# Gate columns of a pooling mixer as seven block products per pair, trailing sums one column later

## The chip, the cores and the metric

The kernel runs on one core of a Trainium2 chip. The metric is device time in microseconds (us) of one execution; the time before is the median of three runs. TensorE (PE in the rows) multiplies, VectorE (DVE) and ScalarE (ACT) prepare its operands and take its results out of PSUM, SyncE (SP) issues the loads. Each of these engines works its own list of instructions in order and waits at semaphores for the others.

## The reference, cut to what matters

Two blocks of a network follow each other on 512 tokens with 1024 features. The change is in the first layer of the second block, the pooling mixer:

```
u = h @ w_in                       # 512 x 4096: 2048 values, 2048 gates
v, gate = split(u, 2)
for g, w in enumerate((2, 4, 8, 16)):          # four groups of 512 channels
    c = cumsum(v)[group g]; cnt = min(pos + 1, w)
    p[g] = (c - c shifted by w tokens) / cnt - v[group g]     # trailing mean minus token
m = p[g] @ w_grp[g] * scale
y = (m * silu(gate)) @ w_out
```

h is the RMS norm of the residual with a gain per feature.

## The kernel before, in words

**Three matmuls per product.** Every float32 operand is split into a high part, rounded to fp32r by ScalarE, and a low part, the rest, by a subtraction on VectorE. A product is high times high, high times low and low times high (`three`, L649 to L651). Activations lie in HH and HL with features on partitions, weights in WH and WL, four slots of 1024 columns each. A weight unit (128 x 1024, 512 KB) lands in one of five places of RAW, ScalarE copies it to WH (`hi_to`, L2375), VectorE subtracts (`lo_to`, L1371) and frees the place in RAW for the next load.

**The pooling mixer** works group after group, g from 0 to 3. Per group TensorE does four value columns ("pv", 128 output channels x 512 tokens over all 1024 features: 24 matmuls with 512 moving columns), four gate columns ("pg", the same shape) and the group product ("pm", 48 such matmuls). In group 0 the values are done in halves of 256 tokens while the second half of h is still being made. For each value column ScalarE copies the PSUM bank to VP (L2819), VectorE makes the trailing sum (`window`, g + 1 additions of a tile and its shifted self, L1898, each of which waits for the one before, then one scaled subtraction L1903 and two short instructions on the first 16 tokens), ScalarE rounds the result (L2809) and VectorE takes its low part (L1913). There is one VP and one result tile PP, so the four windows of a group take turns with ScalarE. A gate column goes through a sigmoid on ScalarE (L2827) and a multiplication on VectorE (L1923). The low part of a window and the multiplication of a gate are put off (`late`) and issued at the next `flush`.

**What sets the order.** Each engine has its own program that walks over the same columns; `column(evac)` issues the splits of the next units and then, at the eighth step, what evac does. A split of unit n + 2 stands in column n, ahead of that column's evacuation.

**The boundary behind fc2** (`boundary`) makes h for the mixer: TensorE transposes two token tiles at a time (L645); for the other two boundaries, out and pout, ScalarE writes the whole value to tile E (`whole`, L2483 or L2485), rounds it to HH (L2502), and VectorE subtracts (L1506). Behind fc2 both read PSUM directly, with the gain in the instruction (L2508, L1508), and E isn't written.

**Seven block products** are in use already in the fc1 stage. A pair of columns of 128 outputs over 1024 features and 512 tokens is taken as 2 x 2 blocks and done with seven products instead of eight (`half_product`, L990 to L992), each 12 matmuls with 256 moving columns. The sums of activation blocks are made once from E (`hidden_sums`, L1769 to L1775, four instructions of 1024 columns), rounded (`hidden_sum`, L2715) and given low parts in ER (`hidden_low`, L1784). Per pair four sums of weight blocks (`weight_sum`, 512 columns) and seven splits of 512 columns are made (L2735 on ScalarE, L1825 on VectorE). The products accumulate in PSUM: some are copied out by ScalarE (L2747, L2750), and VectorE adds three (L1838); a bank's next product waits until that is done. The hgrn value columns behind pout use such products too, with the same helpers; their weight splits are L2865 and L2010.

## Time and profile before

| | |
|---|---|
| median of 3 runs | 1404.72 us (1404.55 to 1405.58) |
| profiled execution | 1405.39 us, of which 1403.6 us from first to last instruction |
| TensorE busy | 1391.3 us (99%) |
| VectorE, ScalarE busy | 981.9 us (70%), 648.3 us (46%) |
| granted TensorE clock | 0.998 of full speed |
| pooling groups 1, 2, 3 begin at | 641.4, 696.1 and 750.8 us |

Matmuls overlap in the rows (one with 512 moving columns is shown with 0.39 us and the next begins well before it ends), so the pace of TensorE is read from start to start. The same holds for VectorE and ScalarE: an instruction that doesn't wait for its predecessor begins before that one's end.

### The profile page before, as it was taken

Reading aid. Unit: us, or ns where it says so; the run is one execution under the profiler, and the core shown is the slowest. Engines: PE = TensorE matmul, PEld = TensorE weight load, DVE = VectorE, ACT = ScalarE, POOL = GpSimd, SP = SyncE. Lnnn points to the kernel's source line nnn. Section 1 sums busy time; section 2 is a strip of 40 time slices with the busy share of each in tenths; the row PEclk is TensorE's granted clock in tenths of the full one; section 3 lists DMA queues with packets and bytes.
Section 4 is the critical chain, followed back from the end, with each engine's and each line's share of the span. In section 5 each row is a group of like instructions: output and inputs, shape, how many; then the busy total and the mean of one; then the engine's idle time right before and its main releaser. Section 6 shows DMA issues by size and latency. Waiting matters only on the chain.

```text
span 1403.6 us, 22088 instructions
## 1 busy us (share of the span) xinstructions
PE 1391.3 (99%) x8666; PEld 1191.6 (85%) x8666; DVE 981.9 (70%) x1922; ACT 648.3 (46%) x1268; POOL 0.2 (0%) x4
## 2 busy tenths in 40 slices
PE   8999999999999999999999999999999999999998
PEld 7888888999998888888888888988888888888886
DVE  7887776799953335655476535499788889888645
ACT  6423355567762324542342323575345555556441
POOL 0000000000000000000000000000000000000000
PEclk9999999999999999999999999999999999999999
DMA  9656441244333224032332234213322222221221
GB/s 359 220 177 250 152 157 70 95 163 154 111 115 99 97 94 161 32 105 91 93 117 75 91 107 148 76 43 112 117 91 76 76 76 78 74 76 61 76 75 60
DMA packets 43734, 158.00 MB, mean 113 GB/s; under 512 B 4848, under 2 KB 5232, under 8 KB 43632
## 3 DMA queue, kind: packets, MB, share of 16 engines
q1 hardware_dynamic: 43344, 156.39, 32.8%
q8 instruction: 69, 1.13, 0.3%
q14 instruction: 33, 0.27, 0.1%
q10 hardware_dynamic: 288, 0.21, 0.0%
HBM read 154.48 MB, written 2.10 MB: 112 GB/s over the span
## 4 chain that ended last, share of the span: by engine, by line
PE 97%; DVE 1%; issue 1%; DMA 0%; ACT 0%; SPq 0%; DVEq 0%; ACTq 0%
PE PS L649 26%; PE PS L651 26%; PE PS L650 26%; PE PS L990 2%; PE PS L992 2%; PE PS L991 2%; PE PS L1046 2%; PE PS L1048 2%; PE PS L1049 2%; PE PS L1147 1%; PE PS L1151 1%; PE PS L645 1%; PE PS L1139 1%; PE PS L1079 1%; PE PS L1160 0%
## 5 line engine op out<-in xcount | busy, mean ns | idle before, releaser
L649 PE MATMUL PS<-HH,WH 128*128 128x512 f32 (+1 forms) x880 | 337.3, 383 | 0.0
L651 PE MATMUL PS<-HH,WL 128*128 128x512 f32 (+1 forms) x880 | 332.8, 378 | 0.0
L650 PE MATMUL PS<-HL,WH 128*128 128x512 f32 (+1 forms) x880 | 332.5, 378 | 0.0
L2375 ACT ACTIVATE WH<-RAW 128x1024 fp32r<-128x1024 f32 x176 | 185.3, 1056 | 133.2 <-PE PS L651 87.0
L1371 DVE TENSOR_TENSOR WL<-RAW,WH 128x1024 fp32r<-128x1024 f32 x176 | 213.8, 1219 | 18.5 <-ACT WH L2375 18.1
L651 PEld LDWEIGHTS PS<-HH,WL 128*128 128x128 f32 x880 | 165.6, 188 | 31.4
L649 PEld LDWEIGHTS PS<-HH,WH 128*128 128x128 f32 x880 | 165.6, 188 | 30.7
L650 PEld LDWEIGHTS PS<-HL,WH 128*128 128x128 f32 x880 | 165.7, 188 | 29.3
L649 PE MATMUL PS<-WH,ZH 128*128 128x512 f32 x400 | 155.9, 390 | 0.0
L651 PE MATMUL PS<-WH,ZL 128*128 128x512 f32 x400 | 155.7, 389 | 0.0
L650 PE MATMUL PS<-WL,ZH 128*128 128x512 f32 x400 | 155.6, 389 | 0.0
L1422 DVE TENSOR_TENSOR ZL<-Z,ZH 128x512 fp32r<-128x512 f32 x52 | 35.6, 691 | 136.4 <-ACT ZH L2440 136.4
L2440 ACT ACTIVATE ZH<-Z 128x512 fp32r<-128x512 f32 x52 | 32.4, 632 | 149.2 <-PE PS L651 149.2
L651 PEld LDWEIGHTS PS<-WH,ZL 128*128 128x128 f32 x400 | 75.1, 188 | 15.7
L649 PEld LDWEIGHTS PS<-WH,ZH 128*128 128x128 f32 x400 | 75.1, 188 | 15.5 <-ACT Z L2750 0.2
L650 PEld LDWEIGHTS PS<-WL,ZH 128*128 128x128 f32 x400 | 75.1, 188 | 15.5
L990 PE MATMUL PS<-HH,WH 128*128 128x256 f32 x192 | 54.4, 283 | 0.3 <-DVE Z L1838 0.3
L992 PE MATMUL PS<-HH,WL 128*128 128x256 f32 x192 | 54.3, 283 | 0.0
L991 PE MATMUL PS<-ER,WH 128*128 128x256 f32 x192 | 54.3, 283 | 0.0
L2062 DVE RECIPROCAL DG<-W 128x96 f32<-128x96 f32 (+1 forms) x64 | 48.9, 815 | 0.0
L2467 ACT ACTIVATE TMP<-X 128x1024 f32<-128x1024 f32 x18 | 19.0, 1056 | 47.8 <-DVE X L1486 29.9
L649 PE MATMUL PS<-WH,HH 128*128 128x512 f32 x96 | 39.0, 407 | 2.0 <-DVE RAW L1331 2.0
(351 smaller groups left out, 2625.6 us busy)
## 6 DMA issues: line engine op xcount, KB each, us to landing
RAW<-in_w_fc SPq DMA_DIRECT2D x64, 512.0 KB, 3.5
RAW<-in_hgrn_in SPq DMA_DIRECT2D x56, 512.0 KB, 3.3
RAW<-in_pool_in SPq DMA_DIRECT2D x40, 512.0 KB, 3.3
RAW<-in_ada SPq DMA_DIRECT2D x36, 512.0 KB, 4.5
RAW<-in_w_in SPq DMA_DIRECT2D x26, 512.0 KB, 5.1
RAW<-in_pool_out SPq DMA_DIRECT2D x16, 512.0 KB, 3.3
RAW<-in_hgrn_out SPq DMA_DIRECT2D x16, 512.0 KB, 3.3
Z<-in_ada SPq DMA_DIRECT2D x12, 512.0 KB, 4.4
```

The costliest lines, as they stand in the source:

```text
L649: e.matmul(out, wh, xh, start=first, stop=False)
L650: e.matmul(out, wh, xl, start=False, stop=False)
L651: return e.matmul(out, wl, xh, start=False, stop=last)
L990: e.matmul(out, wh[:, k, :], xh[k], start=fresh and k == 0, stop=False, skip_group_check=True)
L991: e.matmul(out, wh[:, k, :], xl[k], start=False, stop=False, skip_group_check=True)
L992: mm = e.matmul(out, wl[:, k, :], xh[k], start=False, stop=k == 3, skip_group_check=True)
L1046: e.matmul(out, xh[k][:, cols], wh, start=k == 0 and p in (1, 2, 7), stop=False, skip_group_check=True)
L1371: e.tensor_tensor(lo, raw(i), hi.bitcast(F32), ALU.subtract).then_inc(taken.sem, taken(i))
L1422: e.tensor_tensor(lo, Z[:, k, :], hi.bitcast(F32), ALU.subtract).then_inc(zlo.sem, zlo(z))
L2062: e.reciprocal(i8[:, n, l], w8[:, n, l]).then_inc(own.sem, own("iw", h, i))
L2375: e.activation(place(s)[0], raw(i), ACT.Copy).then_inc(whi.sem, whi(s))
L2440: e.activation(z_place(z)[0], Z[:, k, :], ACT.Copy).then_inc(zhi.sem, zhi(z))
```

## The change

The fc2 boundary now goes through E as the other two do, and `hidden_sums`, `hidden_sum` and `hidden_low` are called for it in group 0. In groups 1 to 3 the four gate columns become two pairs with seven products each, 14 per group (list `POOLED`; the second number of a pair is the pair of columns). Windows 0, 1 and 2 of these groups stand in the evacuation of the following value column, window 3 behind the second product. The additions of a window are as before.

```diff
+POOLED = [(p, 2 * g + n) for g in range(3) for p, n in
+          ((1, 0), (7, 0), (6, 0), (2, 0), (4, 0), (5, 0), (1, 1), (7, 1), (3, 0), (6, 1), (2, 1), (5, 1), (4, 1), (3, 1))]
...
+        def pooled_bank(p, q):
+            return gate_bank(1, {7: 2, 4: 2, 2: 3}.get(p, q % 2))
...
+            def pooled_product(m):
+                i, q = POOLED[m]
+                b = pooled_bank(i, q)
+                claim(b)
+                if i in (3, 5, 6, 7) and q == 0:
+                    e.wait_ge(hidden_high.sem, hidden_high.of("fc2", i))
+                e.wait_ge(taken.sem, taken.of("pooled", m))
...
+                for k in range(4):
+                    e.matmul(out, wh[:, k, :], xh[k], start=fresh and k == 0, stop=False, skip_group_check=True)
+                    e.matmul(out, wh[:, k, :], xl[k], start=False, stop=False, skip_group_check=True)
+                    mm = e.matmul(out, wl[:, k, :], xh[k], start=False, stop=k == 3, skip_group_check=True)
...
-                for j in range(4):
+                for j in range(0 if g else 4):
                     run(column(("pg", g, j), gate_bank(g, j)))
+                if g:
+                    for m in range(14 * g - 14, 14 * g):
+                        pooled_product(m)
+                    p.unit += 4
...
-            boundary("fc2", VEC[:, V_NG0:V_NG0 + 8])
+            boundary("fc2", None)
...
+            def pooled_low(m):
+                i, q = POOLED[m]
+                if i == 5 and q % 2 == 0:
+                    pooled_sum(3, q + 1)
+                if i == 1 and q % 2:
+                    pooled_sum(2, q)
+                if i == 7 and q % 2:
+                    pooled_sum(4, q)
+                if i == 3 and q % 2 == 0:
+                    pooled_sum(1, q + 1)
+                e.wait_ge(copied.sem, copied.of("pooled", m))
+                hi, lo = pooled_place(m)
+                e.tensor_tensor(lo, pooled_source(m), hi.bitcast(F32), ALU.subtract).then_inc(
+                    taken.sem, taken("pooled", m))
...
+            def first_pooled(g, j):
+                q = 2 * g - 2
+                if j == 0:
+                    pooled_sum(3, q)
+                    pooled_sum(2, q)
+                if j == 1:
+                    window(g, 0)
+                    pooled_sum(4, q)
+                    pooled_low(7 * q)
+                    pooled_low(7 * q + 1)
+                if j == 2:
+                    window(g, 1)
+                    pooled_sum(1, q)
+                    pooled_low(7 * q + 2)
+                    pooled_low(7 * q + 3)
+                if j == 3:
+                    window(g, 2)
+                    pooled_low(7 * q + 4)
...
-                    run(halved([[], [lambda j=j: window(0, j) for j in range(4)]]))
+                    run(halved([[], [lambda j=j: window(0, j) for j in range(4)]], lambda: hidden_sums("fc2")))
+                    for j in range(4):
+                        run(column(lambda: pool_gate(0, j)))
+                        hidden_low("fc2", (7, 6, 5, 3)[j])
                 else:
                     for j in range(4):
-                        run(column(lambda: window(g, j)))
-                for j in range(4):
-                    run(column(lambda: pool_gate(g, j)))
+                        run(column(lambda: first_pooled(g, j)))
+                    for m in range(14 * g - 14, 14 * g):
+                        n = m % 14
+                        if n + 5 < 14:
+                            pooled_low(m + 5)
+                        if n:
+                            pooled_taken(*POOLED[m - 1])
+                        if n == 1:
+                            window(g, 3)
+                        if n == 6:
+                            flush()
+                        if n in (7, 11):
+                            pooled_silu(g, (7, 11).index(n))
+                        if n == 10:
+                            p.unit += 4
+                            lo_to(p.unit + 1)
...
+            def pooled_copied(i, q):
+                b = pooled_bank(i, q)
+                if i in (1, 7, 6):
+                    e.wait_ge(*banks.made(("pooled", i, q)))
+                    if q:
+                        e.wait_ge(*banks.taken(("pooled", {1: 2, 7: 5, 6: 4}[i], q - 1)))
+                    e.activation({1: C1, 7: C7, 6: C2}[i], PS[b][:, 0:256], ACT.Copy).then_inc(banks.free[b], 1)
...
+                    for m in range(14 * g - 14, 14 * g + 1):
+                        n = m - 14 * g + 14
+                        if n:
+                            pooled_copied(*POOLED[m - 1])
+                        if n == 4:
+                            pool_high(g, 3)
+                        if n + 6 < 14:
+                            pooled_high(m + 6)
+                        if n in (6, 10, 14):
+                            pooled_sigmoid(g, (6, 10, 14).index(n))
+                        if n == 9:
+                            p.unit += 4
+                            hi_to(p.unit + 2)
```

`pooled_sum` is `weight_sum` for the gate units (3, 2 and 4 write to TMP, 1 to RAW), `pooled_high` is ScalarE's rounding of half a unit, and `pooled_taken` adds a copied product to the bank of products 2, 4 and 5.

On VectorE in group 0, behind the last window (L1898 and L1962 are its addition, L1913 and L1977 its low part), before:

```order
L1898 TENSOR_TENSOR Z<-Z 128x512
L1903 SCALAR_TENSOR_TENSOR Z<-Z 128x496
L1905 TENSOR_TENSOR Z<-Z,CST 128x16
L1908 TENSOR_TENSOR Z<-Z 128x16
L1913 TENSOR_TENSOR ZR<-Z,PSP 128x512
L1371 TENSOR_TENSOR WL<-RAW,WH 128x1024
L1923 TENSOR_TENSOR Z<-Z,PS 128x512
L1371 TENSOR_TENSOR WL<-RAW,WH 128x1024
```

and in the same place after the change (L1433 is the split of a whole unit, L1848 is `hidden_low`, L1987 the gate's multiplication):

```order
L1962 TENSOR_TENSOR Z<-Z 128x512
L1967 SCALAR_TENSOR_TENSOR Z<-Z 128x496
L1969 TENSOR_TENSOR Z<-Z,CST 128x16
L1972 TENSOR_TENSOR Z<-Z 128x16
L1977 TENSOR_TENSOR ZR<-Z,PSP 128x512
L1848 TENSOR_TENSOR ER<-E,ZH 128x256 x2
L1848 TENSOR_TENSOR ER<-E,ZL 128x256 x2
L1433 TENSOR_TENSOR WL<-RAW,WH 128x1024
L1987 TENSOR_TENSOR Z<-Z,PS 128x512
```

Four short subtractions stand ahead of the split that the fourth gate column of group 0 needs.

On VectorE in group 3, from window 3 on, before (window, then splits of whole units and gates in turn):

```order
L1898 TENSOR_TENSOR Z<-Z 128x512 x4
L1903 SCALAR_TENSOR_TENSOR Z<-Z 128x496
L1905 TENSOR_TENSOR Z<-Z,CST 128x16
L1908 TENSOR_TENSOR Z<-Z 128x16
L1371 TENSOR_TENSOR WL<-RAW,WH 128x1024
L1913 TENSOR_TENSOR ZR<-Z,PSP 128x512
L1371 TENSOR_TENSOR WL<-RAW,WH 128x1024
L1923 TENSOR_TENSOR Z<-Z,PS 128x512
L1371 TENSOR_TENSOR WL<-RAW,WH 128x1024
```

and after the change (L1999, L2003, L2006 and L2009 are the weight sums 3, 2, 4 and 1, L2023 the split of half a unit, L2037 is `pooled_taken`):

```order
L1962 TENSOR_TENSOR Z<-Z 128x512 x4
L1967 SCALAR_TENSOR_TENSOR Z<-Z 128x496
L1969 TENSOR_TENSOR Z<-Z,CST 128x16
L1972 TENSOR_TENSOR Z<-Z 128x16
L2006 TENSOR_TENSOR TMP<-RAW,TMP 128x512
L2023 TENSOR_TENSOR WL<-TMP,WH 128x512
L2009 TENSOR_TENSOR RAW<-RAW 128x512
L2023 TENSOR_TENSOR WL<-RAW,WH 128x512
L2023 TENSOR_TENSOR WL<-TMP,WH 128x512
L2037 TENSOR_TENSOR Z<-PS,TMP 128x256
L2023 TENSOR_TENSOR WL<-RAW,WH 128x512
L2037 TENSOR_TENSOR Z<-PS,TMP 128x256
```

The second addition L2037 is that of product (4, 0); it frees the PSUM bank that product (7, 1), the eighth of the group, claims. Two sums and four splits stand between window 3 and it.

## Rows read from the trace of the kernel before

**Rows 1.** The page: TensorE's busy time, and the chain that ended last.
```profile
PE 1391.3 (99%) x8666; PEld 1191.6 (85%) x8666; DVE 981.9 (70%) x1922; ACT 648.3 (46%) x1268; POOL 0.2 (0%) x4
PE 97%; DVE 1%; issue 1%; DMA 0%; ACT 0%; SPq 0%; DVEq 0%; ACTq 0%
```

**Rows 2.** Timeline of TensorE: start us, us, engine, line, operation, out<-in, shape, count.
```profile
641.40 0.39 PE L649 MATMUL PS<-HH,WH 128*128 128x512 f32 x1
684.95 0.40 PE L649 MATMUL PS<-PSP,WH 128*128 128x512 f32 x1
```

**Rows 3.** Timeline of TensorE in the fc1 products.
```profile
339.93 0.28 PE L990 MATMUL PS<-HH,WH 128*128 128x256 f32 x1
342.81 0.28 PE L990 MATMUL PS<-HH,WH 128*128 128x256 f32 x1
```

**Rows 4.** Timeline of VectorE, pooling group 3, first window.
```profile
757.15 2.87 DVE L1898 TENSOR_TENSOR Z<-Z 128x512 f32<-128x512 f32 x4 [3.07 <-ACT Z L2819]
760.94 1.22 DVE L1371 TENSOR_TENSOR WL<-RAW,WH 128x1024 fp32r<-128x1024 f32 x1
```

**Rows 5.** Timeline of VectorE in the fc1 products.
```profile
293.28 0.69 DVE L1825 TENSOR_TENSOR WL<-TMP,WH 128x512 fp32r<-128x512 f32 x1
293.88 0.42 DVE L1838 TENSOR_TENSOR Z<-PS,TMP 128x256 f32<-128x256 f32 x1
294.21 0.68 DVE L1825 TENSOR_TENSOR WL<-RAW,WH 128x512 fp32r<-128x512 f32 x1
```

**Rows 6.** Timeline of ScalarE, pooling group 3.
```profile
761.96 0.60 ACT L2819 ACTIVATE Z<-PS 128x512 f32<-128x512 f32 x1 [3.90 <-PE PS L651]
762.45 0.62 ACT L2809 ACTIVATE PSP<-Z 128x512 fp32r<-128x512 f32 x1
```

**Rows 7.** Busy us and instructions per engine, two stretches.
```profile
core 0: us, PE busy (x) PEld busy (x) DVE busy (x) ACT busy (x) POOL busy (x), PEclk, DMA share, GB/s
320.00:360.00 40.00, 40.00 (x336) 40.00 (x335) 36.19 (x61) 29.03 (x60) 0.00 (x0) 1.00 0.43 145
700.00:760.00 60.00, 60.00 (x265) 49.45 (x264) 35.79 (x58) 19.51 (x25) 0.00 (x0) 1.00 0.32 103
```

**Rows 8.** Timeline of TensorE, a wait in the fc1 products.
```profile
297.76 0.39 PE L990 MATMUL PS<-ZH,WH 128*128 128x256 f32 x1 [0.77 <-ACT TMP L2747]
297.98 0.28 PE L991 MATMUL PS<-ER,WH 128*128 128x256 f32 x1
```

**Rows 9.** Timeline of TensorE, group 0: first matmul of its fourth gate column.
```profile
624.82 0.39 PE L649 MATMUL PS<-HH,WH 128*128 128x512 f32 x1
```

**Rows 10.** Timeline of VectorE, group 0.
```profile
608.28 0.70 DVE L1898 TENSOR_TENSOR Z<-Z 128x512 f32<-128x512 f32 x1
621.13 0.69 DVE L1913 TENSOR_TENSOR ZR<-Z,PSP 128x512 fp32r<-128x512 f32 x1 [0.70 <-ACT PSP L2809]
622.08 1.23 DVE L1371 TENSOR_TENSOR WL<-RAW,WH 128x1024 fp32r<-128x1024 f32 x1 [0.26 <-ACT WH L2375]
```

**Rows 11.** Timeline of ScalarE, group 0.
```profile
621.00 1.04 ACT L2375 ACTIVATE WH<-RAW 128x1024 fp32r<-128x1024 f32 x1
621.95 0.58 ACT L2827 ACTIVATE Z<-PS 128x512 f32<-128x512 f32 x1
```

**Rows 12.** Timeline of TensorE, second transposes behind fc2 and behind pout.
```profile
593.35 0.33 PE L645 MATMUL PS<-CST,Z 128*128 128x128 f32 x1
904.03 0.38 PE L645 MATMUL PS<-CST,Z 128*128 128x128 f32 x2
```

**Rows 13.** Timeline of VectorE behind pout.
```profile
910.73 1.23 DVE L1769 TENSOR_TENSOR E<-E 128x1024 f32<-128x1024 f32 x1
915.64 1.22 DVE L2010 TENSOR_TENSOR WL<-RAW,WH 128x1024 fp32r<-128x1024 f32 x1
916.78 1.43 DVE L1784 TENSOR_TENSOR ER<-E,ZR 128x256 fp32r<-128x256 f32 x4
```

**Rows 14.** Timeline of ScalarE behind pout.
```profile
914.50 1.34 ACT L2715 ACTIVATE ZR<-E 128x256 fp32r<-128x256 f32 x4 [3.35 <-DVE E L1773]
```

More of the change, by code:

```diff
@@ L80, in slot_list @@
 def slot_list():
-    slots, before, last, ring, first, vfirst = [], [], {}, 0, None, None
+    slots, before, last, ring, first, vfirst, pooled = [], [], {}, 0, None, None, []
     for s, i in enumerate(GEMM):
@@ L96, in slot_list @@
                 ring = (first[0] + len(PRODUCTS)) // 2
+            continue
+        if name == "pool_in" and n >= 10 and 4 <= n % 10 < 8:
+            if n % 10 == 4:
+                pooled.append((2 * ring, dict(last)))
+            slots.append(None)
+            before.append(None)
+            if n % 10 == 7:
+                for m in range(14):
+                    last[(pooled[-1][0] + m) % (2 * NS) // 2] = "pooled", 14 * (len(pooled) - 1) + m
+                ring += 7
             continue
@@ L120, in slot_list @@
         last[slot] = s
-    return slots, before, first, vfirst
-SLOT, BEFORE, PFIRST, VFIRST = slot_list()
+    return slots, before, first, vfirst, pooled
+SLOT, BEFORE, PFIRST, VFIRST, GFIRST = slot_list()
 def product_half(m):
@@ L397, in operand @@
                     return h, [l[:, i, :] for i in range(4)]
+                if p == 3 and stage == "fc2":
+                    h = [ZR[:, 30 + i // 2, 256 * (i % 2):256 * (i % 2) + 256] for i in range(4)]
+                    return h, [l[:, i, :] for i in range(4)]
                 if p != 3:
@@ L546, in ready @@
         def ready(stage, p, k):
-            if stage == "fc2" and k >= 4:
-                return banks.taken((stage, "t", p, k - 4))
             return hlo.sem, hlo.of(stage, p, k)
@@ L1001, in tensor_program @@
             rows("fc2", 32)
+            def pooled_product(m):
[5 more added lines that the diff above has]
+                e.wait_ge(taken.sem, taken.of("pooled", m))
+                wh, wl = (x.rearrange("p (k c) -> p k c", k=4) for x in pooled_place(m))
+                xh, xl = operand(i, "fc2")
+                out, fresh = PS[b][:, 0:256], i in (1, 2, 7)
+                for k in range(4):
+                    e.matmul(out, wh[:, k, :], xh[k], start=fresh and k == 0, stop=False, skip_group_check=True)
+                    e.matmul(out, wh[:, k, :], xl[k], start=False, stop=False, skip_group_check=True)
+                    mm = e.matmul(out, wl[:, k, :], xh[k], start=False, stop=k == 3, skip_group_check=True)
+                mm.then_inc(banks.full[b], banks.fill(("pooled", i, q), b))
+                wfree["pooled", m] = banks.made(("pooled", i, q))
             for g in range(4):
@@ L1421, in z_low @@
                     e.wait_ge(*banks.made(("product", 7 - (z - 8), FG - 1)))
+                if ZSTAGE[z] == 2 and z - 40 < NZ:
+                    e.wait_ge(*banks.made(("pooled", {2: 7, 0: 6, 1: 5}[ZSLOT[z]], 5)))
                 e.tensor_tensor(lo, Z[:, k, :], hi.bitcast(F32), ALU.subtract).then_inc(zlo.sem, zlo(z))
@@ L1924, in pool_gate, with pooled_sum @@
                 late.append(last)
+            def pooled_sum(i, q):
+                a, b = pooled_units(q)
+                b11, b21, b12, b22 = (raw(n)[:, c:c + 512] for n in (a, b) for c in (0, 512))
+                if i != 1 and q:
+                    e.wait_ge(taken.sem, taken.of("pooled", POOLED.index(({3: 7, 2: 6, 4: 4}[i], q - 1))))
+                if i == 3:
+                    e.wait_ge(*landed(b))
+                    e.tensor_tensor(PT[3], b22, b12, ALU.subtract).then_inc(own.sem, own("pooled", 7, q))
+                elif i == 2:
+                    e.wait_ge(*landed(a))
+                    e.wait_ge(own.sem, own.of("pooled", 7, q))
+                    e.tensor_tensor(PT[2], PT[3], b11, ALU.add).then_inc(own.sem, own("pooled", 6, q))
+                elif i == 4:
+                    e.wait_ge(own.sem, own.of("pooled", 6, q))
+                    e.tensor_tensor(PT[4], b21, PT[2], ALU.subtract).then_inc(own.sem, own("pooled", 4, q))
+                else:
+                    e.wait_ge(own.sem, own.of("pooled", 7, q))
+                    e.tensor_tensor(b12, b12, b11, ALU.subtract).then_inc(own.sem, own("pooled", 5, q))
@@ new lines, in pooled_silu @@
+            def pooled_silu(g, j):
+                e.wait_ge(gate.sem, gate.of("pg", g, j))
+                e.tensor_tensor(Z[:, 16 + j, :], Z[:, 16 + j, :], pooled_gate(j), ALU.mult).then_inc(
+                    own.sem, own("pg", g, j))
+            def first_pooled(g, j):
[16 more added lines that the diff above has]
+                    pooled_low(7 * q + 4)
@@ L2435, in z_high @@
                     e.wait_ge(*banks.made(("product", 7 - (z - 8), FG - 1)))
+                if ZSTAGE[z] == 2 and z - 40 < NZ:
+                    e.wait_ge(*banks.made(("pooled", {2: 7, 0: 6, 1: 5}[ZSLOT[z]], 5)))
                 if ZSLOT[z] == NZ:
@@ L2710, in hidden_sum @@
                 x, h = quarter(E, k, t), operand(i, stage)[0]
-                if stage == "out" and i == 3:
-                    e.wait_ge(*banks.made(("fc1", FS - 1)))
+                if i == 3 and stage != "pout":
+                    e.wait_ge(*banks.made(("fc1", FS - 1) if stage == "out" else ("pv", 0, 3)))
                 e.wait_ge(own.sem, own.of("sum", stage, i))
@@ L2834, in scalar_program @@
                     run(halved([[], [lambda j=j: pool_values(0, j) for j in range(4)]]))
+                    pool_high(0, 3)
+                    for j in range(4):
+                        run(column(lambda: pool_gate(0, j)))
+                        hidden_sum("fc2", (7, 6, 5, 3)[j])
                 else:
```

91 lines of the change are left out of this document (70 added, 21 removed).

## The prediction, made before the changed kernel ran

> **What bounds the kernel now.** I read the page first: TensorE is busy 1391.3 of 1403.6 us, and the chain that ended last is TensorE for 97% [rows 1]. So the time is the number of matmuls times their pace, and a change pays only by what it takes off TensorE and by waits that it doesn't bring there. Then the timeline of TensorE, start to start. Between 641.40 and 684.95 lie the eight columns of group 1, 192 matmuls with 512 moving columns: 43.55 / 192 = 0.2268 us each [rows 2]. In the fc1 products 24 matmuls with 256 columns take 342.81 - 339.93 = 2.88 us, 0.120 each, 1.44 per product [rows 3]. Last, the timelines of VectorE and ScalarE, which must feed the new products. VectorE has room in the mean (35.79 of 60 us busy in group 2 and the start of group 3 [rows 7]), but a product wait is decided by its place in an in-order list, so I count the list.
>
> **What TensorE saves.** Four gate columns are 96 matmuls x 0.2268 = 21.78 us; 14 products are 168 x 0.120 = 20.16 us. 1.62 us less per group, **4.9 us** in three groups. The number of instructions grows by 216; group 0, the values and the group product stay.
>
> **A rule that speaks against it.** The rows give a short matmul 0.53 of a long one. The Trainium skill, "TensorE: Matmul & The Clock Gate", section "Back-to-back issue gap", gives a stream of weight loads and matmuls about 131 ns at 512 columns and about 81 at 128. By these, as an estimate, 168 matmuls at 81 or more (13.6 us) replace 96 at 131 (12.6), and the change loses at least 1 us per group before any wait. The trace has neither level; I go by the rows.
>
> **Durations of the helpers, start to start.** VectorE: a split or sum of 512 columns 293.88 - 293.28 = 0.60 (0.605 in longer runs), an addition out of PSUM with 256 columns 0.33, 0.42 until it is finished [rows 5]. The four additions of a window take 2.87 to the end of the last, (2.87 - 0.69) / 3 = 0.725 each since each waits for the one before; the whole window of group 3 is 760.94 - 757.15 = 3.79, so w = 0.89 + 0.725 (g + 1): 2.34, 3.07 and 3.79 us in groups 1, 2, 3 [rows 4]. ScalarE: a bank of 512 columns 0.49, the rounding behind it 0.62 until it is finished [rows 6]. A stopped TensorE restarts with one matmul of 0.22 in place of 0.12 [rows 8]: 0.1 us more per wait.
>
> **Groups 1 to 3: the wait of the eighth product.** Time from the group's start. The products begin at 21.78, the eighth, (7, 1), is due at 21.78 + 7 x 1.44 = 31.86. Its PSUM bank is that of (4, 0), freed by a VectorE addition. What stands ahead of that on VectorE: column 1 of the values ends at 10.89, ScalarE starts on it 0.29 later and has rounded window 0 by 11.18 + 0.49 + 0.62 = 12.29. From 12.32 on VectorE has no pause: low part of window 0, window 1, a sum and two splits, low part, window 2, then split, sum, split, sum, split, low part, window 3, sum, split, sum, split, split, the addition of (2, 0), a split, the addition of (4, 0). That is 17 instructions x 0.605 = 10.28, three windows, and 0.33 + 0.42 + 0.03: together 12.32 + 11.06 + 3w = 23.4 + 3w.
> - Group 3: 34.8, 2.9 late. With the restart 3.05. (The third product waits 0.3 for the copy of the first, which ScalarE reaches late; that lies inside the 2.9.)
> - Group 2: 32.6, 0.73 late, with the restart 0.85.
> - Group 1: 30.4, but the split ahead of window 3 waits for its rounding, which ScalarE does behind column 3 (21.78 + 0.29 + 0.49 + 0.52 + 0.62 = 23.7). From there 8 x 0.605 + 2.34 + 0.78 = 7.96, so 31.7: 0.16 early, no wait.
>
> Bounds for this term: nothing if the list is as little late as in the fc1 products, where the longest wait shown is 0.77 [rows 8]; and one more 0.085 per instruction if VectorE needs the full 0.69 shown instead of 0.605, as below. I take the ledger, since its durations come from the same instructions.
>
> **The twelfth product.** (5, 1) claims the bank that ScalarE copies for (6, 1). That copy stands behind the rounding of the second pm unit, whose place in WH is free only when (6, 1) itself is done. So: end + 0.2, 0.95 [rows 11] for the rounding, 0.4 for the copy, 0.06 = 1.6 against the 1.44 of (2, 1) in between: 0.15 plus restart, **0.25 per group**, between nothing and 0.5. Later products, the two sigmoids at the end and the split of the second pm unit fit: about 3.6 us after the last product (5.2 in group 2, where eight short instructions on the next layer's bounds stand ahead) against the 5.57 until it is needed.
>
> **Group 0: the split behind `hidden_low`.** The fourth gate column starts at 624.82 [rows 9]; its weight split starts at 622.08 [rows 10], done 1.5 us before. After the change three things push it.
> - The boundary through E and the four sums. Behind pout the sums start 910.73 - 904.03 = 6.70 after the second transposes and take 915.64 - 910.73 = 4.91 [rows 12, 13]. Behind fc2 that makes 593.35 + 6.70 = 600.05, about 0.45 more for the ScalarE rounding (1.04 [rows 11]) that the split ahead of the sums waits for, that split 1.15, sums 4.91, two splits 2.29: the first window starts at 608.85, not at 608.28 [rows 10], 0.57 late. The four windows alternate with ScalarE, so this stays.
> - ScalarE then does rounding, sigmoid and, new, four copies of a hidden sum: 621.95 + 0.57 + 0.48 = 623.0, and 1.34 for four [rows 11, 14], 624.35.
> - VectorE waits for these and subtracts, four in 1.34 (one alone 0.42, 1.43 to the end of the fourth [rows 13]), to 625.7; only then the split, 1.22 [rows 13], 626.95.
>
> TensorE wants it at 624.82: **2.15 us late**, 2.25 with the restart. Bounds: 1.0 if the ScalarE copies overlap, 3.0 if the boundary is as slow as the one with a shift. The next splits are in time. The boundary itself costs TensorE nothing: it waits for the token norms, as before.
>
> **Sum.** Waits 2.25 + 0.25 + (0.85 + 0.25) + (3.05 + 0.25) = 6.9, saving 4.9: **2.0 us more**. Against the profiled execution (1403.6 span, 1405.39 with what lies around it) that is 1407.4; against the median 1404.72 it is **1406.7**.
>
> **Rivals.**
> - *VectorE keeps pace.* For it: in the fc1 products TensorE is busy 40.00 of 40 us with VectorE at 36.19 [rows 7], and the pooling groups load VectorE less in the mean. Against: no window of 3.8 us stands in that list. Then only the twelfth products wait, 0.75 in all, and the time is 1404.7 - 4.9 + 0.75 = 1400.6.
> - *Slower: VectorE pays full durations.* Place: the same lists. If a sum or split here needs its shown 0.69 [rows 5] because each waits for another engine's semaphore, 17 x 0.085 = 1.4 us come on top in groups 3 and 2, 0.7 in group 1, 0.2 in group 0: 1404.7 + 2.0 + 3.7 = 1410.4. It decides from a spacing of about 0.64, which gives 1408.3. For it: the window additions do pay (0.725). Against: the splits in [rows 5] wait for ScalarE too and are 0.60 apart.
> - *The short matmul costs its shown share.* If the pace went as the durations, 0.28 to 0.39 [rows 2, 3], 168 x 0.72 x 0.2268 = 27.4 per group in place of 21.8, 17 us in all, 1429 with the waits. The page named above leans that way, the trace doesn't.
> - *Only part is done.* The order shows 216 more matmuls and none of the gate columns left in groups 1 to 3, so I give it nothing.
>
> **How the numbers follow.** Forecast 0.6, VectorE keeps pace 0.14, full durations 0.25, shown share 0.01. A measurement of this kernel tells about 0.2% (2.8 us) from no change, so faster is under 1401.9 and slower over 1407.5. The forecast's own range is 1404.8 to 1408.6 (group 0 between 1.0 and 3.0, group 3 between 2.2 and 4): of its 0.6, 0.43 lie within the bound, 0.16 above, 0.01 below. Of 0.14, 0.11 is faster and 0.03 the same; of 0.25, 0.20 is slower and 0.05 the same. Faster 0.12, same 0.51, slower 0.37. The range, with about one in ten left out on each side, is 1402.5 to 1409.8.
>
> **What would show it.** The changed profile should have TensorE idle before a 512-column matmul near 625 us, released by VectorE's whole-unit split, about 2 us; idle before a product with 256 columns some 32 us after the start of groups 2 and 3, released by VectorE's addition from PSUM, near 0.8 and 2.9 us, and none or almost none in group 1; a short one about four products later, released by ScalarE's copy to TMP. Products at 1.44 us each between. I am wrong if these waits are missing (then the first rival), if VectorE's splits stand 0.69 apart (the second), or if TensorE waits elsewhere, at the fc2 transposes above all.

## The result

| | before | after |
|---|---|---|
| median | 1404.72 us | 1408.67 us (11 executions, 1407.87 to 1409.56) |
| profiled execution | 1405.39 us, span 1403.6 | 1409.56 us, span 1407.8 |
| ratio to before | | 1.0027, interval 1.0019 to 1.0035 |

The change costs 3.95 us by these medians, and 3.8 by the ratio. The forecast was 1406.7, which is 2.0 us more than before. The result lies in the range of 1402.5 to 1409.8, and beyond the 0.2% within which I had put my largest chance. The direction and the places were right. The size was not: nearly half of the loss is something that the sum had no term for.

The page of the changed kernel, the rows that answer to [rows 1]:

```profile
PE 1389.9 (99%) x8882; PEld 1199.9 (85%) x8882; DVE 1023.4 (73%) x2014; ACT 676.5 (48%) x1354; POOL 0.2 (0%) x4
PE 91%; DVE 6%; ACT 1%; issue 1%; DMA 0%; SPq 0%; ACTq 0%; DVEq 0%
```

TensorE is busy 1.4 us less and the span is 4.2 us longer, so it now stands still for some microseconds. In the chain VectorE went from 1% to 6%. Where it is shows in busy time by stretch, about group 0 and then groups 1, 2 and 3 (columns as in [rows 7]). First the kernel before, where all four stretches look alike:

```profile
596.00:640.00 44.00, 44.00 (x244) 38.37 (x243) 24.30 (x43) 16.79 (x25) 0.00 (x0) 1.00 0.27 90
...
750.00:810.00 60.00, 60.00 (x265) 49.40 (x264) 39.16 (x56) 19.19 (x26) 0.00 (x0) 1.00 0.29 92
```

and the changed one:

```profile
596.00:640.00 44.00, 41.90 (x224) 36.03 (x223) 32.53 (x63) 22.69 (x46) 0.00 (x0) 0.96 0.25 84
640.00:700.00 60.00, 59.95 (x342) 52.62 (x341) 43.37 (x71) 25.94 (x45) 0.00 (x0) 1.00 0.30 97
700.00:750.00 50.00, 49.43 (x295) 43.91 (x295) 41.46 (x77) 23.08 (x40) 0.00 (x0) 1.00 0.30 97
750.00:810.00 60.00, 57.51 (x323) 50.55 (x323) 46.63 (x77) 24.37 (x43) 0.00 (x0) 0.97 0.29 96
```

Two things are to be seen. TensorE stands still for 2.1, 0.05, 0.57 and 2.49 us. And the granted clock, the third number from the end, was 1.00 in all four stretches before and is 0.96 and 0.97 in the two stretches with the long waits. The chip took the clock down there.

The first of them, in TensorE's timeline (the wait in brackets, then the durations), which answers to [rows 9]:

```profile
626.25 0.50 PE L690 MATMUL PS<-HH,WH 128*128 128x512 f32 x1 [2.10 <-DVE WL L1433]
626.59 0.39 PE L691 MATMUL PS<-HL,WH 128*128 128x512 f32 x1
626.82 0.46 PE L692 MATMUL PS<-HH,WL 128*128 128x512 f32 x1
627.07 0.63 PE L690 MATMUL PS<-HH,WH 128*128 128x512 f32 x1
...
630.06 0.57 PE L691 MATMUL PS<-HL,WH 128*128 128x512 f32 x1
630.46 0.39 PE L692 MATMUL PS<-HH,WL 128*128 128x512 f32 x1
```

From start to start the wait costs 2.26 us over the usual pace and the restart 0.11. From 627.07 to 630.46 eight matmuls take 3.39 us where eight at 0.227 take 1.82: 1.57 us more. In windows of one microsecond the granted clock reads so:

```profile
625.00:626.00 1.00, 0.00 (x0) 0.00 (x0) 1.00 (x2) 1.00 (x4) 0.00 (x0) 1.00 0.00 0
627.00:628.00 1.00, 1.00 (x4) 0.74 (x4) 1.00 (x4) 1.00 (x4) 0.00 (x0) 0.50 0.53 168
...
631.00:632.00 1.00, 1.00 (x6) 0.83 (x5) 1.00 (x2) 0.00 (x0) 0.00 (x0) 1.00 0.87 352
```

TensorE stood still at the upper level (2.4 GHz), took up work again, fell to the lower one (1.2 GHz) 0.8 us after the restart and came back while it was busy. The eighth product of group 3 shows the same with 256 columns, where the spacing grows from 0.12 to 0.21 us half a microsecond after the restart:

```profile
786.86 0.38 PE L1056 MATMUL PS<-ZH,WH 128*128 128x256 f32 x1 [2.27 <-DVE Z L2037]
787.09 0.28 PE L1057 MATMUL PS<-ER,WH 128*128 128x256 f32 x1
...
787.32 0.31 PE L1056 MATMUL PS<-ZH,WH 128*128 128x256 f32 x1
787.44 0.41 PE L1057 MATMUL PS<-ER,WH 128*128 128x256 f32 x1
```

Time over the usual pace, in us, added up over all matmuls of a stretch:

| | forecast | waits and restarts | behind a fallen clock |
|---|---|---|---|
| group 0, fourth gate column | 2.25 | 2.37 | 1.57 |
| group 1, twelfth product | 0.25 | 0.31 | |
| group 2, eighth and twelfth | 0.85 + 0.25 | 0.79 + 0.30 | |
| group 3, third | in the next | 0.43 | |
| group 3, eighth and twelfth | 3.05 + 0.25 | 2.53 + 0.31 | 1.48 |
| sum | 6.9 | 7.04 | 3.05 |

Less 4.9 saved, the waits alone make 2.2 us, and with both falls 5.2 us. The measured median is between, 3.95. The span of this one execution is only 4.2 us longer because all before fc2's second transposes took 0.83 us less: they start at 592.52, not at 593.35 as in [rows 12]. Nearly all of that is a fall of the clock near the start of the kernel, far from the change. The trace of the kernel before has it:

```profile
17.85 0.47 PE L649 MATMUL PS<-WH,HH 128*128 128x512 f32 x1 [2.04 <-DVE RAW L1331]
...
19.43 0.63 PE L649 MATMUL PS<-WH,HH 128*128 128x512 f32 x1
...
20.00:21.00 1.00, 1.00 (x4) 0.81 (x3) 1.00 (x2) 0.97 (x3) 0.00 (x0) 0.50 1.03 410
```

TensorE waits 2.04 us there, and 1.2 us after the restart the clock is at its lower level. The changed kernel has the same wait of 2.04 us, and in this profile no fall behind it. From the restart (17.85 before, 17.75 after) to the first product with ZR (25.84 and 24.98) the fall costs 0.76 us, less than its slow matmuls, because the changed kernel's profile has a wait of 0.64 us behind them (until 21.82) and the other has none there.

### The profile page after: what moved, and what is told of

Its sections match the earlier page's. It is cut to its first block, busy times and chain, and to the rows that moved or that the text cites. A ratio compares the mean times of both kernels' runs of the same rounds, so it can differ in the third digit from the quotient of the medians.

```text
span 1407.8 us, 22809 instructions
## 1 busy us (share of the span) xinstructions
PE 1389.9 (99%) x8882; PEld 1199.9 (85%) x8882; DVE 1023.4 (73%) x2014; ACT 676.5 (48%) x1354; POOL 0.2 (0%) x4
## 4 chain that ended last, share of the span: by engine, by line
PE 91%; DVE 6%; ACT 1%; issue 1%; DMA 0%; SPq 0%; ACTq 0%; DVEq 0%
PE PS L690 23%; PE PS L692 23%; PE PS L691 23%; PE PS L1031 2%; PE PS L1033 2%; PE PS L1032 2%; PE PS L1108 2%; PE PS L1111 2%; PE PS L1110 2%; DVE Z L1962 1%; PE PS L1056 1%; PE PS L1209 1%; PE PS L1057 1%; PE PS L1058 1%; PE PS L1213 1%
## 5 line engine op out<-in xcount | busy, mean ns | idle before, releaser
L690 PE MATMUL PS<-HH,WH 128*128 128x512 f32 (+1 forms) x784 | 301.0, 384 | 2.1 <-DVE WL L1433 2.1
L692 PE MATMUL PS<-HH,WL 128*128 128x512 f32 (+1 forms) x784 | 296.2, 378 | 0.0
L691 PE MATMUL PS<-HL,WH 128*128 128x512 f32 (+1 forms) x784 | 296.0, 378 | 0.0
L2534 ACT ACTIVATE WH<-RAW 128x1024 fp32r<-128x1024 f32 x164 | 172.5, 1057 | 123.9 <-PE PS L692 77.1
L1433 DVE TENSOR_TENSOR WL<-RAW,WH 128x1024 fp32r<-128x1024 f32 x164 | 199.1, 1219 | 17.1 <-ACT WH L2534 16.7
L690 PEld LDWEIGHTS PS<-HH,WH 128*128 128x128 f32 x784 | 147.9, 189 | 29.6 <-DVE WL L1433 2.5
L692 PEld LDWEIGHTS PS<-HH,WL 128*128 128x128 f32 x784 | 148.0, 189 | 27.8
L691 PEld LDWEIGHTS PS<-HL,WH 128*128 128x128 f32 x784 | 148.2, 189 | 25.6
```

The source lines that it names most:

```text
L690: e.matmul(out, wh, xh, start=first, stop=False)
L691: e.matmul(out, wh, xl, start=False, stop=False)
L692: return e.matmul(out, wl, xh, start=False, stop=last)
L1433: e.tensor_tensor(lo, raw(i), hi.bitcast(F32), ALU.subtract).then_inc(taken.sem, taken(i))
L2534: e.activation(place(s)[0], raw(i), ACT.Copy).then_inc(whi.sem, whi(s))
```

## The experiments

All ratios are to the kernel before, timed in turn on the same chip. Its median was 1405.38 us beside the first four experiments, 1405.11 beside the waits put in by hand and the first repeat of the changed kernel, and 1405.48 beside the rest.

**One part of group 0 undone.** The blocks of `hidden_low` one column later:

```diff
                     for j in range(4):
                         run(column(lambda: pool_gate(0, j)))
-                        hidden_low("fc2", (7, 6, 5, 3)[j])
+                        if j:
+                            hidden_low("fc2", (7, 6, 5)[j - 1])
+                    hidden_low("fc2", 3)
```

> The changed kernel, with each block of hidden_low in group 0 issued one column later on VectorE, so that the weight split of the fourth gate column stands ahead of the first block. In the trace of the changed kernel TensorE waits 2.26 us there, restarts with 0.11 more, and the eight matmuls after it start 0.2 us further apart than usual (1.57 us together) while the granted clock is at its lower level. Theory A (the place in VectorE's list makes the wait, and the clock falls because of the wait): wait, restart and slow matmuls all go, 3.9 us less, 1404.7 us. Theory B (the wait goes, but the clock falls near 628 us anyway): 2.4 us less, 1406.3. Theory C (VectorE simply has too much to do there, the wait moves to a later column): within 1 us of the changed kernel, 1408.

Measured: 1405.73 us, ratio 1.0002 (0.9993 to 1.0011), so 3.5 us less than the changed kernel's 1.0027. VectorE in this kernel:

```profile
622.09 1.23 DVE L1433 TENSOR_TENSOR WL<-RAW,WH 128x1024 fp32r<-128x1024 f32 x1 [0.26 <-ACT WH L2536]
623.24 0.68 DVE L1987 TENSOR_TENSOR Z<-Z,PS 128x512 f32<-128x512 f32 x1
623.87 0.76 DVE L1848 TENSOR_TENSOR ER<-E,ZH 128x256 fp32r<-128x256 f32 x2
```

The split stands right behind the low part of the window again, as in [rows 10], and no wait is left in group 0. In the changed kernel it stood behind the four subtractions, and began 4.07 us behind that low part (L1977) and not 0.95, so 3.12 us later:

```profile
620.90 0.69 DVE L1977 TENSOR_TENSOR ZR<-Z,PSP 128x512 fp32r<-128x512 f32 x1 [0.70 <-ACT PSP L2962]
623.62 0.76 DVE L1848 TENSOR_TENSOR ER<-E,ZH 128x256 fp32r<-128x256 f32 x2 [2.03 <-ACT ZL L2868]
624.30 0.75 DVE L1848 TENSOR_TENSOR ER<-E,ZL 128x256 fp32r<-128x256 f32 x2
624.97 1.22 DVE L1433 TENSOR_TENSOR WL<-RAW,WH 128x1024 fp32r<-128x1024 f32 x1
```

VectorE idles 2.03 us for ScalarE's copies while a split that it could do waits in line. Theory C falls: nothing moved to a later column. Theory A and theory B differ only in the clock behind 628 us, which is up in this profile. Something else is to be seen: group 3 still has its wait of 2.44 us over the pace, in the profile with the clock up.

```profile
783.07 0.39 PE L1056 MATMUL PS<-ZH,WH 128*128 128x256 f32 x1 [2.28 <-DVE Z L2037]
...
783.53 0.29 PE L1056 MATMUL PS<-ZH,WH 128*128 128x256 f32 x1
```

The eleven executions lie in two clusters, five from 1403.96 to 1404.92 and six from 1405.73 to 1406.39; the profiled one belongs to the lower. So the same wait may have a fall behind it in one execution and none in the next. That is not shown: no execution of the upper cluster was profiled, and the fall near 20 us, which the profiled one doesn't have either, is a second thing that can differ (worth 0.8 us, where the clusters lie some 1.8 apart).

**Window 3 later.** Behind the addition of (4, 0) and (5, 0) instead of ahead of them:

```diff
-                        if n == 1:
-                            window(g, 3)
-                        if n == 6:
-                            flush()
+                        if n in (1, 13):
+                            flush()
+                        if n == 6:
+                            window(g, 3)
...
-                        if n == 4:
+                        if n == 11:
                             pool_high(g, 3)
```

> The changed kernel, with window 3 of groups 1 to 3 moved on VectorE from behind the second product's split to behind the addition of product (5, 0), its rounding on ScalarE behind the copy of the tenth product, and its low part behind the thirteenth step. Theory A (list place): the waits of the eighth product, 0.69 + 0.1 in group 2 and 2.43 + 0.1 in group 3, go, and with the latter about 1.5 us of slow matmuls behind it; the twelfth product's waits and the 0.33 at the third stay. 4.8 us less than the changed kernel, 1403.9. Theory B (slow matmuls are not due to the wait): 3.3 less, 1405.4. Theory C (VectorE has too much to do in group 3, its window of 3.8 us only shifts the wait to products 12 to 14 or to the group product): less than 1.5 us gained, 1407.2 or more.

Measured: 1404.2 us, ratio 0.9994 (0.9985 to 1.0002), 4.6 us less than the changed kernel. VectorE in group 3:

```profile
781.32 0.41 DVE L2037 TENSOR_TENSOR Z<-PS,TMP 128x256 f32<-128x256 f32 x1
781.65 0.67 DVE L2023 TENSOR_TENSOR WL<-RAW,WH 128x512 fp32r<-128x512 f32 x1
782.25 0.41 DVE L2037 TENSOR_TENSOR Z<-PS,TMP 128x256 f32<-128x256 f32 x1
782.59 2.85 DVE L1962 TENSOR_TENSOR Z<-Z 128x512 f32<-128x512 f32 x4
```

The waits of the eighth product are gone in both groups, and none came in their place: what is left in groups 2 and 3 is 0.31, 0.43 and 0.30 us. So the wait comes not from the amount of VectorE's work but from the place of 3.8 us of it. Group 0 keeps its 2.27 us wait, this time with a granted clock of 1.00 behind it in the profile. The time alone can't tell theory A from theory B (4.6 us less, where they say 4.8 and 3.3, and the two ratios leave 1.6 us either way); the trace shows that wait and slow matmuls are both gone.

**Both, and the rounding of the second pm unit behind the copy of (6, 1).**

```diff
                             p.unit += 4
-                            hi_to(p.unit + 2)
+                            hi_to(p.unit + 1)
+                        if n == 10:
+                            hi_to(p.unit + 2)
```

> Both of these moves, and ScalarE's rounding of the second unit of the group product behind the copy of the tenth product instead of ahead of it, so that the twelfth product's bank is free in time (three waits of 0.2 + 0.1). Theory A: 3.9 + 4.8 + 0.9 less than the changed kernel, 1399.1; with what stays (0.4 at the third product of group 3) it would be the 4.9 us saved on TensorE less 0.5, near 1400. Theory C: the waits come back elsewhere, 1404 or more.

Measured: 1400.75 us (five executions within 1399.96 and 1401.03), ratio 0.9969 (0.9956 to 0.9981). One wait is left in the four groups:

```profile
772.64 0.39 PE L1056 MATMUL PS<-ZH,WH 128*128 128x256 f32 x1 [0.17 <-ACT TMP L3003]
```

The twelfth products wait no more. The 4.9 us saved less 0.43 make 4.5; the ratio gives 4.4. The 3.9, 4.8 and 0.9 that I had added up to 1399.1 held both falls in full, which the median of the changed kernel doesn't.

**Work for TensorE in its waits.**

```diff
+            def fill(b, n):
+                claim(b)
+                for _ in range(n):
+                    e.matmul(PS[b][:, 0:256], HH[:, 0, 0:128], HH[:, 0, 0:256], start=True, stop=True,
+                             skip_group_check=True)
...
                 for j in range(0 if g else 4):
+                    if j == 3:
+                        fill(gate_bank(0, 3), 17)
                     run(column(("pg", g, j), gate_bank(g, j)))
...
                     for m in range(14 * g - 14, 14 * g):
+                        if m == 35:
+                            fill(pool_bank(3, 0), 19)
                         pooled_product(m)
```

> The changed kernel with work for TensorE in its two long waits: 17 matmuls of 256 columns into a PSUM bank that nobody reads, ahead of the fourth gate column of group 0 (2.0 of 2.26 us), and 19 ahead of the eighth product of group 3 (2.3 of 2.43 us). The lists of the other engines are unchanged, so the columns behind start when they did. Theory A (the clock falls because TensorE stands still): the granted clock stays at its upper level behind both places, 1.6 + 1.5 = 3.1 us less, 1405.6. Theory B (the clock falls for another reason, or from TensorE's load): no change, 1408.7, and the same eight slow matmuls.

Measured: 1406.88 us, ratio 1.0013 (1.0004 to 1.0022). The lists of the other engines are the same, the column and the product start as long after their predecessors as they did (to 0.03 us in group 0), and yet the time is 2.0 us less than the changed kernel's. Nine of eleven executions lie between 1406.56 and 1407.76; two took 3581 and 6526 us, for which I have no cause. TensorE in group 0:

```profile
624.06 0.39 PE L692 MATMUL PS<-HH,WL 128*128 128x512 f32 x1
624.29 2.19 PE L1048 MATMUL PS<-HH 128*128 128x256 f32 x17
626.57 0.50 PE L690 MATMUL PS<-HH,WH 128*128 128x512 f32 x1
626.90 0.39 PE L691 MATMUL PS<-HL,WH 128*128 128x512 f32 x1
```

With useless matmuls in the waits the clock stayed up behind both places. For group 0 one profile says little, since three of four profiles of the changed kernel have no fall there either; for group 3 all four have it. All nine usual executions lie below the fastest one of the changed kernel (1407.76 and 1407.87). So the fall in group 3 needs TensorE to stand still, and the falls are worth about 2.0 us in the changed kernel's median (the two ratios' intervals leave 0.3 to 3.7), not the 3.1 of its first profile.

**A wait put into the kernel before.** Ahead of the split of the fourth gate column of group 0, n subtractions into a tile that nobody reads (the expectations call them additions), with n = 4, 5 and 10; with 4:

```diff
                     e.wait_ge(whi.sem, whi.of(s))
+                    if UNITS[i][0] == "pool_in" and UNITS[i][1] == 7:
+                        for _ in range(4):
+                            e.tensor_tensor(S2[:, 16:PADW], raw(i)[:, 0:512], hi.bitcast(F32)[:, 0:512],
+                                            ALU.subtract).then_inc(own.sem, own())
+                            e.wait_ge(own.sem, own.n)
```

> The kernel before the change, with one wait put into it by hand: ahead of the weight split of the fourth gate column in group 0 VectorE does four additions on an unused tile (128x512, each waits for the one before, 0.725 us apart as in a window). The split was done 1.5 us before it was needed, so TensorE should stand still for 4 x 0.725 - 1.47 = 1.4 us, plus 0.1 of restart. If the wait costs only itself: 1.5 us more than before. If the granted clock falls behind a wait of this length: about 1.5 us on top in the executions in which it falls. The waits of 0.69 us in the changed kernel's traces show no fall, so I expect few falls or none: 1.5 us more, the executions within 1 us of each other.

> The same with five additions: TensorE should stand still for 5 x 0.725 - 1.47 = 2.15 us, as it does in group 0 of the changed kernel. In five profiles of kernels with waits of this size (two places each) the clock fell behind some and not behind others. If the fall comes with the wait, with a chance: 2.3 us more than before in one part of the executions and 3.9 in the other, in two clusters. If the clock has nothing to do with the wait: 2.3 us in all.

> The same with ten additions: a wait of 10 x 0.725 - 1.47 = 5.8 us. If the fall depends on how long TensorE stands still, the clock now falls in every execution, and all lie in one cluster: 5.9 us for wait and restart and 1.6 or more for slow matmuls, 7.5 to 8.5 us more than before. If it is independent of the wait's length, as with five additions: two clusters.

| n | wait in the profile | restart and slow matmuls | median | over before | executions |
|---|---|---|---|---|---|
| 4 | 1.45 us | 0.11 | 1406.65 | 1.54 (1.0010) | 1405.88 to 1406.95 |
| 5 | 2.18 us | 0.11 | 1407.69 | 2.58 (1.0018) | 1406.66 to 1408.63 |
| 10 | 5.81 us | 2.5 | 1413.9 | 8.8 (1.0064) | 1413.83 to 1414.22 |

With 1.45 us the wait costs itself, 1.56. With 5.81 us the clock is down before TensorE starts again:

```profile
629.00:630.00 1.00, 0.00 (x0) 0.00 (x0) 0.97 (x2) 0.00 (x0) 0.00 (x0) 0.64 0.00 0
630.00:631.00 1.00, 0.10 (x1) 0.10 (x1) 1.00 (x2) 0.00 (x0) 0.00 (x0) 0.50 0.00 0
635.00:636.00 1.00, 1.00 (x4) 0.81 (x3) 0.00 (x0) 0.00 (x0) 0.00 (x0) 0.50 0.98 229
636.00:637.00 1.00, 1.00 (x5) 0.79 (x5) 0.00 (x0) 0.00 (x0) 0.00 (x0) 0.94 0.90 348
```

and the five executions agree to 0.4 us, as the first theory had it. Their 8.8 us are somewhat above its 7.5 to 8.5. With 2.18 us no clear pair of clusters came out, only a spread of 2.0 us with a median 0.3 over the 2.28 that the profile without a fall shows.

**Further profiles of the same two kernels.**

> The changed kernel again, for a second profile and eleven more executions. Its waits must be the same to 0.05 us, since the lists are. If the slow matmuls come by chance of the execution, this profile may show them behind the wait of group 0, behind the eighth product of group 3, behind both or neither, and the time is 2.2 us over before plus 1.5 for each. If they belong to the kernel, they are in the same two places again.

> The changed kernel, one more profile: the waits of 2.26 and 2.44 us must be there again. Whether the matmuls behind them are slow was so once in group 0 and twice in group 3, of two profiles each; if chance of the execution decides, this differs from one profile to the next while the waits stay.

> As the one before: the same waits, and behind each the clock fallen or not.

> The kernel before with the wait of 2.18 us put in by hand, one more profile. In the first the clock stayed up. Its eleven executions reach from 1406.66 to 1408.63 us, 2 us, so some must have had the fall; this one shows it or not.

Measured: 1408.86 us (eight executions, ratio 1.0027, 1.0017 to 1.0037) for the first, and single executions of 1408.98, 1408.75 and 1407.51. In the changed kernel each wait came out the same to 0.02 us in all four profiles. TensorE's restart in group 0 in the third of them:

```profile
627.22 0.50 PE L690 MATMUL PS<-HH,WH 128*128 128x512 f32 x1 [2.10 <-DVE WL L1433]
...
628.02 0.40 PE L690 MATMUL PS<-HH,WH 128*128 128x512 f32 x1
```

Counted over all profiles with a wait of 2.2 to 2.5 us: in group 0 the clock fell behind one of seven (one of four in the changed kernel, none in window 3 later and in the two with five additions). It fell where the wait ended at 626.25, and not in the six where it ended between 627.0 and 627.5. In group 3 it fell in all four of the changed kernel, where the wait ends between 786.1 and 786.9, and not in the one where it ends at 783.1. So the length of the wait alone does not decide; the moment at which it comes may have a part. The profiles differ in one thing more: the one with the fall in group 0 has no fall near 20 us, and the six without have it. It is also why its wait ends almost 1 us earlier than in the repeats. Of the 14 profiles of all kernels, 11 have the fall near 20 us, and 3 of these 11 have it already at 14 to 15 us, behind a wait of only 0.9 us in a stretch where TensorE does small matmuls.

**The copy of the first product ahead of the rounding.** On ScalarE, behind all of the moves above:

```diff
+                        if n == 1:
+                            pooled_high(m + 5)
-                        if n + 6 < 14:
+                        if n and n + 6 < 14:
                             pooled_high(m + 6)
```

> The kernel with both moves and the later rounding of the second unit of the group product, and on ScalarE the copy of a group's first product ahead of the rounding of the seventh half instead of behind it. The last wait that its predecessor shows is the third product of group 3, 0.33 + 0.10 us. If that copy's place makes it, it goes: 0.4 us less than the predecessor's 0.9969 of before, about 1400.4 against a before of 1405.1, that is all of the 4.9 us that TensorE saves. If the rounding put off by 0.4 us is late for VectorE, a wait of a few tenths appears at products 7 to 9 instead.

Measured: 1400.35 us, ratio 0.9963 (0.995 to 0.9977). Group 3 and its values in this kernel:

```profile
750.00:810.00 60.00, 60.00 (x345) 52.89 (x344) 49.40 (x80) 26.08 (x45) 0.00 (x0) 1.00 0.34 106
```

The 0.4 us against the kernel before it is less than the two ratios can tell apart; that the wait of the third product is gone, the trace shows. TensorE stands still nowhere in the four groups, at the upper clock throughout, with VectorE at 49.40 of 60 us: more in the same time than in the changed kernel. This version beats both, by 5.1 and by about 9 us.

## Why the prediction came out as it did

**The saving was right.** From 666.38 to 686.84 group 1 does its 14 products, 20.46 us with a wait of 0.31 in them, so 20.15 against 20.16. The last kernel, which has no waits, is 0.37% under before: 5.1 us where the sum says 4.9. The pace behind it, as in [rows 2, 3]:

```profile
666.38 0.28 PE L1056 MATMUL PS<-HH,WH 128*128 128x256 f32 x1
666.50 0.28 PE L1057 MATMUL PS<-HL,WH 128*128 128x256 f32 x1
...
686.84 0.39 PE L690 MATMUL PS<-PSP,WH 128*128 128x512 f32 x1
```

The rival with the short matmul at its shown share is out with that. By the estimate from the figures of the Trainium skill, "TensorE: Matmul & The Clock Gate", section "Back-to-back issue gap", the change would have lost at least 1 us per group before any wait; the trace doesn't agree, with 0.120 and 0.227 us a matmul.

**The ledger of VectorE was right.** In group 3 it said that (4, 0) is added at 34.8 us from the start of the group. The products of that group begin at 773.93, which puts its start at 752.14, and the addition (the second L2037, 0.42 long) ends at 786.81, so 34.7. VectorE's rows there, which answer to [rows 4, 5], with window 3 ahead of the sums and splits:

```profile
778.67 2.86 DVE L1962 TENSOR_TENSOR Z<-Z 128x512 f32<-128x512 f32 x4
...
782.45 0.69 DVE L2006 TENSOR_TENSOR TMP<-RAW,TMP 128x512 f32<-128x512 f32 x1
...
786.39 0.42 DVE L2037 TENSOR_TENSOR Z<-PS,TMP 128x256 f32<-128x256 f32 x1
```

Group 2 came out at 32.5 for 32.6 (730.07 + 0.41 from 697.99), and in group 1 there is no wait, as said. Sums and splits stand 0.60 apart and not 0.69, so the rival of full durations did not happen, though its 1410.4 is a little nearer to the measured time (1.7 us off) than my forecast (2.0). A time that fits doesn't show a cause: the trace shows none of its spacing.

**Group 0 was right but for a tenth.** Its split was forecast for 625.7 in the time of the kernel before; it starts at 624.97 in an execution whose second transposes come 0.83 earlier than in [rows 12] (592.52), so at 625.8. The wait is 2.26 for 2.15. The boundary behind fc2 cost TensorE nothing, as said: its 16 second transposes take 1.73 us before (from 593.35) and 1.72 after (from 592.52), with no wait around them.

**The twelfth product was right** (0.31 for 0.25 each). ScalarE in group 1, where rows of the same two kinds as in [rows 6, 11] follow each other:

```profile
681.04 1.07 ACT L2534 ACTIVATE WH<-RAW 128x1024 fp32r<-128x1024 f32 x1 [0.17 <-PE PS L1058]
682.01 0.36 ACT L3001 ACTIVATE TMP<-PS 128x256 f32<-128x256 f32 x1
```

The rounding of the pm unit (L2534) waits for TensorE's tenth product, and the copy (L3001) stands behind it. That copy frees the bank for the twelfth product, which starts at 682.42. That wait and that of the third product of group 3 end when the experiments move what stands ahead of ScalarE's copy.

**The rival in which VectorE keeps pace** named about the time that the kernel has once places in VectorE's and ScalarE's lists are changed: 1400.6, against 1400.75 and 1400.35. That is in part luck, since its 0.75 for the twelfth products is not in those two. Against it I had put the window of 3.8 us in the list, and moving just that window took the waits of the eighth products away.

**The step that failed is the sum.** It read "Waits 2.25 + 0.25 + (0.85 + 0.25) + (3.05 + 0.25) = 6.9", and charged each wait with its length and 0.1 for one slow matmul. That was read off a wait of 0.77 us [rows 8], and I took over the small price without bounding the large one. The rows that I quoted don't show what follows a wait of 2 us, but the trace of the kernel before did: its wait of 2.04 us at 17.85 has the clock at 0.50 behind it, so the term could have been asked for. The missing term is the granted clock: 1.57 us in group 0 when it falls, 1.48 in group 3. As an estimate from the four profiles of the changed kernel, a fall in one of four and in four of four makes 0.25 x 1.57 + 1.48 = 1.9 us, and 2.2 + 1.9 = 4.1 where 3.95 was measured. The filled waits, without a fall in the profile, gave 1.8 us over before where the sum of waits gives 2.2.

**Profile by profile the terms add up.** From the span of the kernel before, 1403.6 with the fall near 20 us, I take the 4.9 saved, and 0.8 more where that fall is missing, and add the waits, restarts and slow matmuls that the trace shows in the four groups:

| profile | fall near 20 us | waits and restarts | behind falls | worked out | span |
|---|---|---|---|---|---|
| changed kernel, first | no | 7.0 | 3.05 | 1408.0 | 1407.8 |
| changed kernel, three repeats | yes | 7.1 | 1.5 | 1407.3 | 1407.1, 1407.2, 1407.0 |
| `hidden_low` later | no | 4.7 | 0 | 1402.6 | 1402.6 |
| window 3 later | yes | 3.7 | 0 | 1402.4 | 1402.4 |
| both and the rounding | yes | 0.4 | 0 | 1399.1 | 1399.0 |
| waits filled | no | 7.1 | 0 | 1405.0 | 1405.1 |
| copy of the first product ahead | yes | 0 | 0 | 1398.7 | 1398.9 |

So no further cost of the change is left to find above 0.3 us. Like against like, with the fall near 20 us in both, the changed kernel is 3.4 to 3.6 us longer: 2.2 of waits less the saving and 1.5 of clock in group 3 make 3.7.

The Trainium skill has the mechanism in "TensorE: Matmul & The Clock Gate", section "HAM oscillation — how this bites in real kernels": TensorE that waited long enough is throttled again and starts its next tile cold. The trace agrees for the wait of 5.81 us, with 0.50 granted at the restart. Behind the waits of 2.26 and 2.43 us the first profile shows 0.50 as well, but only after TensorE had run at the upper level for 0.8 and 0.5 us. The Trainium skill, same page, section "What's actually happening", calls the watcher free-running, not started with the kernel; that fits that equal waits had a fall in some executions and not in others, but no run here shows the watcher itself.

**What stays open.** Why the fall came in four of four profiles in group 3 and in one of seven in group 0 isn't settled: the two places differ in moment, in columns, and in that the group 3 wait of the changed kernel follows another one. Why the fall near 20 us comes in 11 of 14 profiles isn't either. The executions of the kernel before reach from 1404.44 to 1406.08 us, and its only profile, 1405.39, has that fall; whether the faster ones lack it isn't shown, and a ratio of medians can be off by some tenths of a microsecond through it. The two clusters of the first experiment are put down to a fall in group 3 without a profile of an upper execution.

## What to carry to other kernels

In an in-order list, count what stands ahead of the one short instruction that frees a buffer or feeds the next step, whatever the engine's share of busy time is, and put behind it what is long (a window of 3.8 us) or waits for another engine (four subtractions that held up a ready split by 3.1 us). Here the changed places took 9 us off the changed kernel, where the new products save 4.9. A wait of TensorE can also cost more than its length. In the four groups those of 1.45 us and less cost themselves and 0.1 us, and those of 2.2 to 2.5 us another 1.5 us in part of the executions, which a forecast needs as a term and in its range. Before you price a wait, look in the trace at hand for one of its size, wherever it stands, and at the granted clock behind it.

## What the hardware showed that I had not expected

- The granted clock can fall after TensorE has taken up its work again: 0.50 in 627 to 628 us, with the restart at 626.25. It doesn't always take that long: in the second profile of the changed kernel the clock was down at the restart of group 3 (0.56 in 786 to 787 us). The rows to look at are those behind the wait.
- The price of a fall hardly depended on the shape: 1.57 us with matmuls of 512 columns and 1.48 with 256. Near 20 us it cost 0.8 net, because it took the place of a wait that came after it.
- Two waits made by hand in one place, 1.45 and 5.81 us, cost 1.5 and 8.8 us in all.
